# Delta rule on TensorE: four levels of a block inverse as 32x32 products instead of 64x64

## The reference: what is computed

```python
a_strict = jnp.einsum("bhnid,bhnjd->bhnij", k_beta, k) * decay * strict
t_inv = lax.linalg.triangular_solve(eye + a_strict, eye, left_side=True, lower=True, unit_diagonal=True)
u = jnp.einsum("bhnij,bhnjd->bhnid", t_inv, v_beta)
w = jnp.einsum("bhnij,bhnjd->bhnid", t_inv, k_beta * jnp.exp(g)[..., None])
...
v_new = u_c - jnp.einsum("bhcd,bhde->bhce", w_c, S)
```

## Time and profile before

| | us |
|---|---|
| median of three runs | 2994.28 |
| lowest and highest run | 2991.57, 3001.99 |
| profiled execution, first to last instruction | 2990.1 |
| TensorE busy in it, multiplications | 2817.9 (94%) |
| DVE, ACT, POOL busy in it | 1814.3, 1181.2, 1144.1 |

### The profile page before, as it was taken

The page is one execution under the profiler, slowest core; times in us unless marked ns, Lnnn a source line. Parts: engine busy times, 40 slices in busy tenths (PEclk is TensorE's granted clock), DMA queues, the critical chain, the costliest instruction groups (busy, mean ns, idle before and its releaser), DMA issues. The chain is left out here.

```text
span 2990.1 us, 48834 instructions
## 1 busy us (share of the span) xinstructions
PE 2817.9 (94%) x18995; PEld 2440.4 (82%) x18995; DVE 1814.3 (61%) x2759; ACT 1181.2 (40%) x2210; POOL 1144.1 (38%) x1213
## 2 busy tenths in 40 slices
PE   7998979997999899998999599999999999999999
PEld 7997779996888688887788478888788888788887
DVE  3226834443555587777796677777887777543544
ACT  3226722223545365555443433333433333332321
POOL 2535930004776200001553456666666666100000
PEclk9999989997999899999999799999999999999999
DMA  8975953225454022221575633333533333654554
GB/s 269 354 251 171 263 166 111 67 74 130 108 147 87 22 75 91 85 68 40 179 246 164 216 93 105 95 103 94 190 105 99 101 105 97 240 170 146 192 167 142
DMA packets 403278, 421.07 MB, mean 141 GB/s; under 512 B 34075, under 2 KB 325995, under 8 KB 401000
## 3 DMA queue, kind: packets, MB, share of 16 engines
q1 hardware_dynamic: 368400, 298.61, 33.5%
q10 hardware_dynamic: 19944, 66.63, 6.8%
q0 software_dynamic: 14704, 52.69, 5.4%
HBM read 257.51 MB, written 160.34 MB: 140 GB/s over the span
## 5 line engine op out<-in xcount | busy, mean ns | idle before, releaser
L3526 PE MATMUL fu_pM<-fu_us_hi,fu_w_ring 128*128 128x512 f32 x2464 | 772.6, 393 | 15.2 <-DVE fu_us_lo L3361 14.3
L3526 PEld LDWEIGHTS fu_pM<-fu_us_hi,fu_w_ring 128*128 128x128 f32 x2464 | 466.3, 189 | 120.5 <-DVE fu_us_lo L3361 17.0
L3526 PE MATMUL fu_pM<-fu_us_lo,fu_w_ring 128*128 128x512 f32 x1232 | 482.8, 392 | 0.0
L3526 PEld LDWEIGHTS fu_pM<-fu_us_lo,fu_w_ring 128*128 128x128 f32 x1232 | 233.4, 189 | 47.8
L3262 ACT ACTIVATE fu_w_ring<-fu_sw 128x512 fp32r<-128x512 f32 x176 | 110.9, 631 | 325.3 <-PE fu_pM L3526 264.1
L3368 DVE TENSOR_TENSOR fu_w_ring<-fu_sw,fu_w_ring 128x512 fp32r<-128x512 f32 x132 | 139.4, 1056 | 65.4 <-ACT fu_w_ring L3262 65.3
L3368 DVE TENSOR_TENSOR fu_w_ring<-fu_w_raw,fu_w_ring 128x512 fp32r<-128x512 f32 x88 | 108.5, 1233 | 104.3 <-ACT fu_w_ring L3262 104.3
L2995 PE MATMUL fu_pM<-fu_us_hi,fu_w_ring 128*128 128x512 f32 x666 | 169.3, 391 | 1.3 <-DVE fu_w_ring L2918 1.3
L3262 ACT ACTIVATE fu_w_ring<-fu_w_raw 128x512 fp32r<-128x512 f32 x132 | 83.0, 629 | 191.3 <-PE fu_pM L3526 169.9
L3409 DVE SCALAR_TENSOR_TENSOR fu_acc<-fu_gb,fu_taps,fu_acc 128x1024 f32<-128x1024 f32 x88 | 133.0, 1513 | 37.7 <-ACT fu_acc L3303 36.9
L2075 ACT ACTIVATE at_pt_hi<-at_pT 128x512 fp32r<-128x512 f32 (+3 forms) x176 | 92.7, 539 | 143.6 <-PE at_pT L2340 142.7
(11 more groups left out here) (539 smaller groups left out, 7141.5 us busy)
## 6 DMA issues: line engine op xcount, KB each, us to landing
fu_w_ring<-scr_gs ACTq DMA_DIRECT2D x37, 704.0 KB, 4.6
fu_w_raw<-in_w_gate SPq DMA_DIRECT2D x22, 1024.0 KB, 5.4
fu_w_raw<-in_w_up SPq DMA_DIRECT2D x22, 1024.0 KB, 5.4
scr_gs<-fu_sg SPq DMA_DIRECT2D x84, 256.0 KB, 3.0
scr_gs<-fu_acc SPq DMA_DIRECT2D x63, 256.0 KB, 2.9
fu_us_lo<-scr_gs ACTq DMA_DIRECT2D x19, 704.0 KB, 4.6
pj_wd<-in_w_down POOLq DMA_DIRECT2D x11, 1024.0 KB, 9.3
scr_td<-pj_td POOLq DMA_DIRECT2D x11, 1024.0 KB, 8.0
```

The costliest lines, as they stand in the source:

```text
L3526: p = pe.matmul(bank(2 * n + m, i)[:, :], a[:, k, :], x[:, k, :], start=(k == 0 and n_pass == 0), stop=(k == HALVES_K - 1 and n_pass == 2))
```

## The change

Levels 1 to 4 never leave the 32x32 diagonal blocks of a 64x64 matrix. Their products are cut from two pieces of 64 rows (`HALVES`) into four pieces of 32 rows and 32 columns (`SUB`), one on each of the four diagonal 32x32 tiles of the array. The last level keeps its 64x64 products and writes to a quarter of the bank of its own, `pQ_last`, so that the parts of `pQ` off the 32x32 blocks stay zero: DVE clears them once at the start of the stage, and TensorE waits for that. The copies of ACT and the additions of DVE keep their sizes.

```diff
+        pQ_last = [p[:, 3 * P:4 * P].rearrange("p (u n) -> p u n", u=2) for p in pX]
+        SUB = [(slice(b * 32, b * 32 + 32), slice(b % 2 * 32, b % 2 * 32 + 32)) for b in range(4)]
+        WHOLE = [(rows, slice(0, C2)) for rows in HALVES]
+        def pieces(lv):
+            return SUB if lv < STEPS else WHOLE
...
         def _(dve):
+            for c in range(2):
+                dve.memset(pX[c][:, 0:3 * P], 0.0).then_inc(p_clear, 1)
...
                         if lv == STEPS:
-                            x, q = x[:, :, 1, :], q[:, :, 1, :]
+                            x, q = x[:, :, 1, :], pQ_last[c]
...
             pe.wait_ge(state_clear, 1)
+            pe.wait_ge(p_clear, 2)
...
-                            for rows in HALVES:
-                                m = pe.matmul(pP[c][rows, un % 2, :], nt[s][rows, lv - 1, un, :], xx[s][rows, un, 0, :],
+                            for rows, cols in pieces(lv):
+                                m = pe.matmul(pP[c][rows, un % 2, cols], nt[s][rows, lv - 1, un, cols], xx[s][rows, un, 0, cols],
                                               start=True, stop=True)
...
                             if lv < STEPS:
-                                for rows in HALVES:
-                                    pe.matmul(pQ[c][rows, un % 2, 0, :], xx[s][rows, un, 1, :], pr[rows, un, :], start=True, stop=True)
-                            for rows in HALVES:
-                                m = pe.matmul(pQ[c][rows, un % 2, 1, :], pr[rows, un, :], xx[s][rows, un, 1, :], start=True, stop=True)
+                                for rows, cols in pieces(lv):
+                                    pe.matmul(pQ[c][rows, un % 2, 0, cols], xx[s][rows, un, 1, cols], pr[rows, un, cols], start=True,
+                                              stop=True)
+                            for rows, cols in pieces(lv):
+                                to = pQ[c][rows, un % 2, 1, cols] if lv < STEPS else pQ_last[c][rows, un % 2, cols]
+                                m = pe.matmul(to, pr[rows, un, cols], xx[s][rows, un, 1, cols], start=True, stop=True)
```

More of the change, by code:

```diff
@@ L1398, in stage_delta @@
         u_done, w_done, u_out, w_out = (r.sems(x) for x in ("u_done", "w_done", "u_out", "w_out"))
+        p_clear = r.sem("p_clear")
         ws, v_ready, ks, s_ready, o_done, o_out, stored = (
```

## The result

The changed kernel takes 3055.24 us (median of 4 runs, 3051.69 to 3061.39) against 2994.55 for the kernel before (now four runs): a ratio of 1.0207, 95% interval 1.0191 to 1.0223. It is slower by 2.1%; the forecast was 2974 us. The profiled execution has a span of 3056.5 us, where before's has 2990.1: 66.4 us more.

What follows compares the result with a forecast made beforehand. TensorE was taken as the bound of the delta rule stage; section gains of 0.19 + 0.40 + 0.12 + 0.40 + 0.11 + 0.40, less 0.45 for shape changes, gave 1.17 us a tile, 19.9 over 17 tiles: 2974 us, range 2965 to 2998 (8 in 10: up to 3002).

Steps and rivals of the forecast that it cites:

- Handing out: TensorE, levels 1 to 4: instructions handed out at 7 to 14 ns a pair; 10.5 taken for sections straight after a wait.
- Smaller products: Levels 1 to 4: 96 pairs for 48 a level; four diagonal tiles work at once, a pass taking 33 ns for 58.
- The tile: One tile of the delta rule's loop: 16.4 us for 17.55, 1.17 us saved in each of 17 tiles.
- Shape changes: Three new changes of array shape a tile, at L1800, turn and second(4): 3 x 0.15 = 0.45 us, bounds 0 and 0.45.
- Memsets: Two of 128x384 on DVE ahead of its first sum: no cost, hidden in idle time; 1.4 us once if not.
- handing out decides: Rival, levels 1 to 4: 384 pairs a tile limited by handing out; 3038 us at 20 ns a pair, chance 0.14.
- The clock: Rival: more idle time from predict(0) to second(2) brings that part to 1.2 GHz; 3000 us, chance 0.07.
- The pass does not shrink: Rival: a tile needs 58 ns a pass whatever its columns, only the shape changes remain; 3002 us, chance 0.07.
- waits take it: Rival: DVE's additions and ACT's copies swallow half a section more in each level; 2988 us, chance 0.06.

Runs made afterwards that it cites:

- pad64: Kernel before, all products 64x64, with an unread product of the same size ahead of each one of levels 1 to 3; 3032.32 us, ratio 1.0132.
- two_levels: Changed kernel with the 32x32 pieces in levels 1 and 2 alone; 3008.94 us, ratio 1.0059 to the kernel before.
- one_level: Changed kernel with the 32x32 pieces in level 1 alone; 2993.34 us, ratio 1.0001 to the kernel before.
- half_pieces: Changed kernel with pieces 0 and 2 alone in levels 1 to 4, the other half of these products left out; 3003.68 us, ratio 1.0039 to before.
- half_slim: half_pieces with 3 wide unread products a tile, one behind each second of levels 1 to 3; 3008.35 us, ratio 1.0058 to the kernel before.
- corners: last_small with the X0 products of level 4 also cut to 32x32, one for one; 3002.01 us, ratio 1.0039 to the kernel before.
- last_small: Kernel before with only the last level cut to its 32x32 corner block, one product for one, its evictions half as wide; 2988.55 us, ratio 0.9986.
- half_wide: half_pieces with 15 wide unread products a tile (64x64 by 192 columns) in levels 1 to 3; 3055.67 us, ratio 1.0211 to the kernel before.

## Why the prediction was wrong

The step that failed is **Handing out**. It asked how fast pairs can follow one another and bounded that by 7 and 14 ns from bursts of 4 and 32 pairs. The answer was right for a burst: 8.4 ns in the changed kernel, and 8.8 in `second(1)`, under the 10.5 taken there. It didn't ask how fast instructions reach the sequencer over a whole tile. The row for that was on the page of before: 153 instruction packets. At 720 a tile, before uses 2.8 blocks of some 256 in 17.55 us, one each 6.2 us; the change asks for 4.3 in the forecast 16.4, one each 3.8 us, and where the changed kernel stops, a block takes 3.98 us (the one from 854.39) to 6.6 to be replaced. So the sum had no term for it. `pad64` shows the term, with the falls of the clock that come with its stops, free of the new shape (1.3% at 1008 instructions, none of them 32x32), `two_levels` and `one_level` show it fading at 912 and 816, and `half_pieces` shows it all but gone at 720.

In size: the changed kernel lies 81 us above the forecast. Its tile from 770 to 1010 us is 5.2 us longer than the forecast 16.4; 3.9 of these are idle time of TensorE (42.8 of 240 us, in a tile of 21.63), and the rest goes with the lower clock, which falls at the stops. Against `half_pieces`, whose sections are nearly as long and whose clock is as low, the added instructions cost 51.6 us. What `half_pieces` itself has above the forecast, 30 us, is a second thing that the sum held at nothing (the forecast gave it a chance of 0.07), the clock under thin work: from 785 to 980 us its tiles (from one start of the final products to the next) take 15.81 to 16.00 us where the clock stays up, and 17.2 to 21.3 where it falls. Its 17.65 is 1.8 above the 15.81, 31 us over 17 tiles. That a loss of this kind is also in the changed kernel, which does twice these products, is not shown; all its falls in the loop lie at stops.

The other steps, in their order:

- *Smaller products* held: a pass over four pieces takes 33 ns (four pairs of 8.4), so all four tiles work at once. The rule of the Trainium skill (TensorEngine Tiling (Array Packing), section Instruction Overhead), some 60 cycles for each product, one column taking as long as 60, does not agree with this across tiles: at 2.4 GHz a pair would take 25 ns, an estimate from that page. It spoke against this change and the change did lose, but not in this way.
- *The tile* of 16.4 us held where nothing disturbs it, as far as kernels with half the pieces show it: 15.81 in `half_pieces`, 16.56 with the three fillers of `half_slim`. The changed kernel has no such tile in its loop.
- *Shape changes* at 0.15 us held: `corners` pays 0.15 to go from 64x64 to 32x32, the pair of shapes that no row of before had, and some 0.12 to go back.
- *Memsets* cost next to nothing. The two take 0.79 us together, and the stage's first product starts at 695.86 instead of 695.37, where the work ahead of the stage is already 0.34 late.

Of the rivals, *handing out decides* was right that it would be slower (3038 at 20 ns a pair) and wrong in its mechanism: no pair takes 20 ns; blocks of some 126 pairs come late. Its chance of 0.14 rested on the pace of bursts, which answers another question. *The clock* put its fall behind predict(0), and there `half_pieces` does fall; in the changed kernel the falls lie at the stops instead. That its 3000 us is close to `half_pieces`' 3003.68 is in part luck, since that kernel leaves out half of the products. *The pass does not shrink* and *waits take it* did not happen.

Open: how low the changed kernel's clock would be without its stops; why less data traffic shortens them; and why `half_pieces` and `half_slim` spread over 31 and 26 us from run to run where before's runs beside them stay within 11 and 6.

## What to carry to other kernels

Splitting products into smaller ones pays in tiles of the array but is paid for in instructions: count them per iteration, divide by those in one instruction packet, and compare the time that this leaves for one packet with what the trace shows (3.8 us was too short here, 6.2 us was enough). A pace read from a burst of 30 pairs says nothing about a thousand instructions. Where a product can be cut one for one, with no change of shape inside a section, the short form does gain, if little (`last_small`, 0.14%).

## What the hardware showed that was not expected

- TensorE stops for up to 3.2 us for want of instructions. The trace names nothing but "issue" as the cause; the signs are that the stops lie whole multiples of 256 instructions apart (27 stops in the changed kernel) and that each ends 1.2 to 1.7 us after a 16 KB packet of the instruction queue. With less than half the data traffic the idle time shrinks by 30% (29.9 against 42.8 us of 240), which points to a resource that loads and code share.
- The granted clock fell to 0.50 in a loop in which TensorE was idle for at most 0.6 us at a time (`half_pieces`), and stayed at 1.00 in the same loop with 15 wide products in it (`half_wide`). In the changed kernel each of eleven falls began in a stop or within 1.8 us behind one, and so did each of five in `pad64`, whose products are not thin.
- Four diagonal 32x32 tiles take pairs 8.4 ns apart, while one change between 64x64 and 32x32 costs 0.12 to 0.15 us, as much as 14 to 18 such pairs.
